# Queries and keys turned and split by the projection, and full-depth score products in the prompt attention

## What the reference computes

```python
def diff_attend(q, k, v, q_pos, k_pos, rel_bias, lam):
    qs = q.reshape(bsz, tq, h, 2, DIFF_DH)          # two maps of 64
    ks = k.reshape(bsz, tk, h, 2, DIFF_DH)
    s = jnp.einsum('bqhmd,bkhmd->bhmqk', qs, ks).astype(F32) * (DIFF_DH ** -0.5)
    rel = q_pos[:, None] - k_pos[None, :]
    bias = jnp.moveaxis(rel_bias.astype(F32)[t5_bucket(rel)], -1, 0)
    s = jnp.where(rel >= 0, s + bias[None, :, None], jnp.finfo(F32).min)
    p = jax.nn.softmax(s, axis=-1)
    a = p[:, :, 0] - lam * p[:, :, 1]
    return jnp.einsum('bhqk,bkhd->bqhd', a, v.astype(F32))
```

## Time and profile before

| what | us |
|---|---|
| median of three runs | 3699.82 (3698.76 to 3701.97) |
| the profiled execution, its own time | 3702.15 |
| span of the profile (first to last instruction) | 3700.1 |
| projection 2, second pass | about 364 |
| prompt attention | about 770 |
| mean granted TensorE clock | 0.967 of full |

### The profile page before, as it was taken

One profiled execution on the slowest core, in us unless ns is written; L12 is line 12 of the kernel. 1 busy time (PEld: TensorE's weight loads), 2 busy tenths in 40 slices (PEclk: granted clock), 3 DMA queues, 4 the chain that ended last, 5 costly groups with the idle time before them and its releaser, 6 DMA issues. The chain is left out here.

```text
span 3700.1 us, 54274 instructions
## 1 busy us (share of the span) xinstructions
PE 3428.9 (93%) x19183; PEld 2764.3 (75%) x19183; DVE 1649.9 (45%) x3504; ACT 1077.4 (29%) x1792; POOL 267.3 (7%) x539
## 2 busy tenths in 40 slices
PE   8999997996899997999999989999999968499999
PEld 6888996774688886888888867777777755278887
DVE  3222201555555553222300028788888733455554
ACT  2111101332211212111200017677777622311111
POOL 0000001110000000000000002112122100000000
PEclk9999998998899999999999989999999978799999
DMA  5433443335322214433422341111111099522221
GB/s 211 150 121 116 142 137 115 119 108 180 135 79 87 78 61 175 153 129 124 149 95 93 104 117 41 45 39 49 48 48 31 14 358 348 199 73 83 80 78 49
DMA packets 218236, 421.99 MB, mean 114 GB/s; under 512 B 20685, under 2 KB 111606, under 8 KB 218054
## 3 DMA queue, kind: packets, MB, share of 16 engines
q1 hardware_dynamic: 218070, 419.89, 32.7%
HBM read 281.51 MB, written 140.14 MB: 114 GB/s over the span
## 5 line engine op out<-in xcount | busy, mean ns | idle before, releaser
L320 PE MATMUL in_ps_y<-in_w_hi,in_x_hi 128*128 128x512 f32 (+2 forms) x2040 | 770.9, 378 | 10.9 <-DVE in_w_lo L423 5.5
L322 PE MATMUL in_ps_y<-in_w_lo,in_x_hi 128*128 128x512 f32 (+2 forms) x2040 | 768.0, 376 | 0.0
L324 PE MATMUL in_ps_y<-in_w_hi,in_x_lo 128*128 128x512 f32 (+2 forms) x2040 | 767.8, 376 | 0.0
L320 PEld LDWEIGHTS in_ps_y<-in_w_hi,in_x_hi 128*128 128x128 f32 x2040 | 384.7, 189 | 75.1 <-issue 11.7
L324 PEld LDWEIGHTS in_ps_y<-in_w_hi,in_x_lo 128*128 128x128 f32 x2040 | 384.4, 188 | 64.1
L322 PEld LDWEIGHTS in_ps_y<-in_w_lo,in_x_hi 128*128 128x128 f32 x2040 | 384.5, 188 | 62.6
L1821 DVE TENSOR_SCALAR_CACHE_REDUCE att_s<-att_ps_s,att_far 128x256 f32<-128x256 f32 (+3 forms) x608 | 331.9, 582 | 34.4 <-PE att_ps_s L1626 30.9
L441 DVE COPY in_out<-in_ps_y 128x512 f32<-128x512 f32 (+1 forms) x85 | 55.8, 657 | 604.9 <-PE in_ps_y L324 604.9
L1664 PEld LDWEIGHTS att_ps_o<-att_v,att_a_t 128*128 128x128 f32 x2176 | 264.2, 191 | 61.8 <-issue 52.0
L1664 PE MATMUL att_ps_o<-att_v,att_a_t 128*128 128x128 f32 x2176 | 308.3, 285 | 0.5 <-ACT att_o L1730 0.5
L1709 ACT ACTIVATE att_s<-att_s,att_shift 128x128 f32<-128x128 f32 (+15 forms) x256 | 306.4, 1199 | 3.4 <-DVE att_shift L1841 3.4
(11 more groups left out here) (246 smaller groups left out, 4731.8 us busy)
## 6 DMA issues: line engine op xcount, KB each, us to landing
smp_k_pg<-in_cache_k SPq DMA_DIRECT2D x64, 512.0 KB, 7.1
smp_v_pg<-in_cache_v SPq DMA_DIRECT2D x64, 512.0 KB, 6.8
x_turned<-in_x_hi SPq DMA_DIRECT2D x34, 512.0 KB, 5.1
x_turned<-in_x_lo SPq DMA_DIRECT2D x34, 512.0 KB, 5.8
factors<-in_out SPq DMA_DIRECT2D x68, 256.0 KB, 2.0
in_x_hi<-x_turned SPq DMA_DIRECT2D x34, 512.0 KB, 4.3
in_x_lo<-x_turned SPq DMA_DIRECT2D x34, 512.0 KB, 5.1
res_factors<-factors SPq DMA_DIRECT2D x34, 512.0 KB
```

The lines of the kernel that those rows point to most:

```text
L320: nc.tensor.matmul(ps_y[g][:, cols], x_hi[u][:, k, :], w_hi[g][:, k, cols], start=(k == 0), stop=False)
L322: nc.tensor.matmul(ps_y[g][:, cols], x_hi[u][:, k, :], w_lo[g][:, k, cols], start=False, stop=False)
L324: mm = nc.tensor.matmul(ps_y[g][:, cols], x_lo[u][:, k, :], w_hi[g][:, k, cols], start=False, stop=(k == KD - 1))
```

## The change

The second pass of projection 2 turns and splits q and k itself. After a group is copied to `out`, PE turns it in four 128x128 transposes into `ps_t` (`turn_again`, placed between two groups of products), ACT writes the high part (scaled for q), DVE the low part, both into halves of the buffers `xt`, which the second pass doesn't use, and SyncE stores both parts turned to four new scratch tensors (1024 x 2048 each; `store_turned`). The stores of q as it is go, but for the samples' tile. In the attention, `prep`, `high`, `low` and `load_nat` go; a head is loaded by twelve DMAs (`load_parts`) into stacked tiles: for each map, `q_hl` holds the high part of q in partitions 0 to 63 and the low part in 64 to 127, `k_hh` the high part of k twice, `k_ll` the low part twice. Scores of a piece are two products of full depth for each map. The handover of scores is by map instead of by pair, and `TURN_RING` becomes 4.

```diff
@@ project
+    def turn_waits(n, t, g):
+        if n == 1 and g in turn:
+            if not (isinstance(t, int) and t == 0):
+                return TURNS * t + g + 1 - TURNS
+        return None
...
+        def re_part(part, n):
+            return xt[part][:, n % 2 * BANK:(n % 2 + 1) * BANK]
...
+                def store_turned(t, g):
+                    sp.wait_ge(re_lo_done, after(TURNS * t + g + 1))
+                    stand_alone(sp, core)
+                    head = turn[g][3]
+                    for part in range(2):
+                        dst = turn[g][part].rearrange("(h p) n -> p h n", p=P)[:, head:head + BANK // P, bass.ds(t * P, P)]
+                        sp.dma_start(dst, re_part(part, g).rearrange("p (h n) -> p h n", n=P)).then_inc(re_kept[g % 2], 16)
+                def stores(n, t):
+                    if n and turn and not (isinstance(t, int) and t == 0):
+                        store_turned(t - 1, G[n] - 1)
+                    for g in range(G[n]):
+                        if not (n and g in turn and not turn[g][4]) or isinstance(t, int) and t == LAST:
+                            store(n, t, g)
+                        if n and turn and g >= 1 and not (isinstance(t, int) and t == LAST):
+                            store_turned(t, g - 1)
...
+                def turn_again(t, g):
+                    n = TURNS * t + g
+                    pe.wait_ge(out_done[g], after(so_far(1, g) + t + 1))
+                    pe.wait_ge(re_lo_done, after(n - 1 if not (isinstance(t, int) and n < 2) else 0))
+                    for b in range(BANK // P):
+                        mm = nc.tensor.transpose(ps_t[g % 2][:, b * P:(b + 1) * P], out[g][:, b * P:(b + 1) * P],
+                                                 core.ident[:, :])
+                    mm.then_inc(re_turned, 1)
...
+                        if n and turn:
+                            if g == 1 and not (isinstance(t, int) and t == 0):
+                                turn_again(t - 1, G[n] - 1)
+                            if g >= 2 and not (isinstance(t, int) and t == LAST):
+                                turn_again(t, g - 2)
...
+                    if n and turn and not (isinstance(t, int) and t == LAST):
+                        turn_again(t, G[n] - 2)
...
+                def high_again(t, g):
+                    act.wait_ge(re_turned, after(n + 1))
...
+                    nc.scalar.activation(re_part(0, g).bitcast(F32R), ps_t[g % 2][:, :], ACT.Copy,
+                                         scale=turn[g][2]).then_inc(re_hi_done, 1)
...
+                def low_again(t, g):
+                    dve.wait_ge(re_hi_done, after(n + 1))
+                    nc.vector.scalar_tensor_tensor(re_part(1, g).bitcast(F32R), ps_t[g % 2][:, :], turn[g][2],
+                                                   re_part(0, g), ALU.mult, ALU.subtract).then_inc(re_lo_done, 1)
@@ attention
-    SLOTS, ROW_RING, TURN_RING = 5, 4, 8
+    SLOTS, ROW_RING, TURN_RING = 5, 4, 4
...
-        k_hi = [sb(f"k_hi{u}", [P, SEQ], F32R) for u in range(2)]
-        k_lo = [sb(f"k_lo{u}", [P, SEQ], F32R) for u in range(2)]
-        q_hi = [sb(f"q_hi{u}", [P, SEQ], F32R) for u in range(2)]
-        q_lo = [sb(f"q_lo{u}", [P, SEQ], F32R) for u in range(2)]
+        k_hh = [[sb(f"k_hh{u}{m}", [P, SEQ], F32R) for m in range(2)] for u in range(2)]
+        k_ll = [[sb(f"k_ll{u}{m}", [P, SEQ], F32R) for m in range(2)] for u in range(2)]
+        q_hl = [[sb(f"q_hl{u}{m}", [P, SEQ], F32R) for m in range(2)] for u in range(2)]
...
+                def load_parts(h, u):
+                    for m in range(2):
+                        for dst, (top, low) in ((q_hl, q_parts), (k_hh, (k_parts[0], k_parts[0])),
+                                                (k_ll, (k_parts[1], k_parts[1]))):
+                            for half, src in enumerate((top, low)):
+                                sp.dma_start(dst[u][m][half * D_DH:(half + 1) * D_DH, :].bitcast(F32),
+                                             src[bass.ds(h * D_VD + m * D_DH, D_DH), :]).then_inc(parts_in[u], 16)
...
-                for g in range(4):
-                    load_nat(0, g)
+                load_parts(0, 0)
                 load_head(0, 0)
-                for g in range(4):
-                    sp.wait_ge(s["turned"], after(2 * g + 2))
-                    load_nat(1, g)
...
                         sp.wait_ge(s["piece_free"], after(PIECES * H + SLOTS))
                         stand_alone(sp, core)
+                        load_parts(H + 1, 1 - u)
                         load_head(H + 1, 1 - u)
                     for i in range(T):
...
-                        if i % 4 == 3 and not (isinstance(H, int) and H + 2 >= D_HEADS):
-                            sp.wait_ge(s["turned"], after(PREPS * (H + 1) + i // 2 + 1))
-                            stand_alone(sp, core)
-                            load_nat(H + 2, i // 4)
...
-                    if c == 0:
-                        pe.wait_ge(s["lo_done"], after(PREPS * H + 2 * (i // 4 + 1)))
-                    pe.wait_ge(s["piece_free"], after(PIECES * H + 2 * at + 2))
-                    for q_part, k_part in ((q_hi, k_hi), (q_hi, k_lo), (q_lo, k_hi)):
-                        for m in range(2):
-                            rows = slice(m * D_DH, (m + 1) * D_DH)
+                    if at == 0:
+                        pe.wait_ge(parts_in[u], after(need_parts(H, u)))
+                    for m in range(2):
+                        pe.wait_ge(s["piece_free"], after(PIECES * H + 2 * at + m + 1))
+                        for k_part in (k_hh, k_ll):
                             mm = nc.tensor.matmul(ps_s[(2 * at + m) % SLOTS][:, 0:hi_ - lo_],
-                                                  q_part[u][rows, i * P:(i + 1) * P], k_part[u][rows, lo_:hi_],
-                                                  start=(q_part is q_hi and k_part is k_hi), stop=(q_part is q_lo))
-                    mm.then_inc(s["piece_ready"], 1)
+                                                  q_hl[u][m][:, i * P:(i + 1) * P], k_part[u][m][:, lo_:hi_],
+                                                  start=(k_part is k_hh), stop=(k_part is k_ll))
+                        mm.then_inc(s["piece_ready"], 1)
```

More of the change, by code:

```diff
@@ L50 @@
 REV = 384
+HEAD_SCALE = -(D_DH ** -0.5)
 class Core:
@@ L122, in so_far, with kept_tiles @@
         return TILES * sum(g < G[a] for a in range(n))
+    turn = turn or {}
+    TURNS = len(turn)
+    def kept_tiles(g):
+        return 1 if g in turn and not turn[g][4] else TILES
+    def turn_waits(n, t, g):
[3 more added lines that the diff above has]
+        return None
     with ExitStack() as mem:
@@ L224, in later_pass @@
                     load_again(t + 1, u)
-                    for g in range(G[n]):
-                        store(n, t, g)
+                    stores(n, t)
                 load_x(0, 0)
@@ L269, in _ @@
                 load_again(1, 0)
-                for g in range(G[1]):
-                    store(1, 0, g)
+                stores(1, 0)
                 with sp.Fori(0, TILES // 2 - 1) as j:
@@ L275, in _ @@
                 later_pass(1, TILES - 2, 1)
-                for g in range(G[1]):
-                    store(1, LAST, g)
+                stores(1, LAST)
                 if beside:
@@ L280, in _ @@
                 for g in range(SLOTS):
-                    sp.wait_ge(stored[g], after(16 * so_far(NP, g)))
+                    sp.wait_ge(stored[g], after(16 * (so_far(1, g) + (kept_tiles(g) if g < G[1] else 0))))
+                for i in range(2 if turn else 0):
+                    sp.wait_ge(re_kept[i], after(32 * LAST * TURNS // 2))
             @block.gpsimd
@@ L398, in _, with again_tile @@
                         weights_high(first_piece[1] + 2 * g + 1)
-                with act.Fori(0, TILES) as t:
+                def high_again(t, g):
+                    n = TURNS * t + g
+                    act.wait_ge(re_turned, after(n + 1))
+                    first = isinstance(t, int) and t == 0
+                    act.wait_ge(re_kept[g % 2], after(0 if first and g < 2 else 32 * (TURNS // 2 * t + g // 2)))
+                    nc.scalar.activation(re_part(0, g).bitcast(F32R), ps_t[g % 2][:, :], ACT.Copy,
+                                         scale=turn[g][2]).then_inc(re_hi_done, 1)
+                def again_tile(t):
                     for g in range(G[1]):
                         evict(1, t, g)
+                        if turn and g == 0 and not (isinstance(t, int) and t == 0):
+                            high_again(t - 1, G[1] - 1)
+                        if turn and g >= 1 and not (isinstance(t, int) and t == LAST):
+                            high_again(t, g - 1)
+                again_tile(0)
+                with act.Fori(1, LAST) as t:
+                    again_tile(t)
+                again_tile(LAST)
             @block.vector
@@ L1486, in bank_uses @@
                 break
```

(23 more changed lines are left out.)

87 lines of the change are left out of this document (41 added, 46 removed).

## The result

The changed kernel takes 3916.47 us (median of four runs, 3911.01 to 3922.61) against 3699.29 beside it: ratio 1.0585, interval 1.0573 to 1.0598, slower by 217 us. 3877 was forecast, +177.5; the time lies outside the forecast's own stretch (3845 to 3905), inside the range (3735 to 3945), and nearest to the rival *half the ports* (3933). The profiled execution took 3922.61 us, its span is 3920.9.

A forecast was written before the change was run, and what follows sets the result against it. It took the projection's second pass as bound by PE alone and prompt attention as mixed, PE or DVE by rows. 28.5 - 40 + 48 + 109 + 22 + 10 = +177.5 us gave 3877; range 3735 to 3945.

The forecast's parts named there:

- half the ports: Rival, chance 0.20: the attention's loads of 64 partitions move only 210 GB/s; total +233 us, time 3933.
- part 1: Second pass of the second projection: 256 transposes added to PE, paid uncovered; +28.5 us.
- first load of the attention: First head's start: loading parts, v and bias at 273 GB/s delays the attention; +13.8 us.
- parts 2 and 3: Attention: four full-depth score products replace six, and turning inside it goes; -5 us a head, -40 in all.
- part 4: Rows 12 to 15 of each head: PE waits for ACT's copies in the smaller ring; +6 us a head, +48.
- part 5: Attention: row 2's output waits for row 0's store behind the loads; 18.1 us a head, +109 in six heads.
- clock after the stalls: Attention: PE restarts at half clock after each stall, an estimated 1.5 us each; +10 us.
- Stores pass the loads: Rival, chance 0.09: stores in the attention aren't held behind loads, so no stall; +50 us, time 3750.
- full rate: Rival, chance 0.14: the attention's loads move 418 GB/s, stalls are shorter; total +116 us, time 3816.
- doesn't do what it says: Rival without its own chance: full-depth score products run no faster, losing 3 us a head; +20 on any case.
- Faster: Rival, chance 0.09: attention rows win back PE and DVE time with the ring's wait hidden; -42 us, time 3658.
- The sign for being wrong: Attention: output waits under 5 us a head, or rows without a stall shorten by over 6 us a head.

The follow-up runs named there:

- e9: Only the projection's turning, splitting and storing of q and k, with the attention of the kernel before: 3731.65 us, ratio 1.0076 to the kernel before.
- e1: Changed kernel with the next head's twelve half loads spread behind the stores of rows 0 to 9: 3731.88 us, ratio 1.0088 to the kernel before.
- e6: Changed kernel with both the loads spread over the rows and five tiles in the ring: 3670.39 us, ratio 0.9918 to the kernel before.
- e8: e6 with the score products of the kernel before (six of 64 rows) and their four loads: 3677.21 us, ratio 0.9938 to the kernel before.
- e3: Changed kernel with five tiles of turned probabilities in the ring instead of four: 3846.10 us, ratio 1.0395 to the kernel before.
- e10: Changed kernel with v, bias and far of heads 1 to 7 issued ahead of the twelve half loads instead of behind them: 3918.18 us.

## Why the prediction was right, and where it was not

The direction and the chain of causes were right: the stall, its place and its releaser, the ring's bubbles and the uncovered turns. The sizes were not, and the time fell outside the forecast's own 3845 to 3905. By steps:

| step | forecast, us | measured, us |
|---|---|---|
| part 1, turns in the projection | +28.5 | +30.6 (trace), +29.7 (e9) |
| first load of the attention | +13.8 | +19.6 |
| parts 2 and 3, over all heads | -40 | about -82 |
| part 4, ring of 4 | +48 | +61.5 (e1 to e6) |
| part 5, held stores | +117 | +184.6 (changed to e1) |
| clock after the stalls | +10 | not seen behind the stalls |
| sum | +177.5 | +217 in the runs; these rows give 213 |

The -82 is made from heads of before and e6: 9.6 in the first (row 0 to row 15), six times 11.8, 2.2 in the last. The +19.6 is from the first load to the first output, 44.9 against 25.3; most of what it has over the forecast is the rate, below. Beside the runs that are set against each other the kernel before took 3697.8 to 3702.8, so these rows are good to a few us.

**The rate** is the step of part 5 that failed. I took 273 GB/s as the mean of three half-microseconds, and they were peaks; the longer stretch, 210 over 2.5 us, was the right row and stood as a rival with 0.20. At 221, v and the parts take 33.8 us, the store lands 36.6 after the first load, and a head pays 118.82 - 90.86 = 28.0 where I had 18.1. About 7 us of the 10 are the rate; row 2 was also due 2.3 us sooner after that load (6.1 instead of 8.4), in part because prep is gone, and the slack behind the stall (a mean wait of 29.3 in heads 1 to 6) is 29.3 - 28.0 = 1.3 instead of 2.6. The sentence of the Trainium skill (SBUF — State Buffer, "Door 1: The DMA port swizzle" and "Can I just issue two DMAs to hit both halves?") that I weighed beside a rival, on half of the ports and on two loads to the two halves, is borne out: the halves alternate between the two sides of the partitions here and still move 221 GB/s, somewhat above its 196 at 1 MB, and 415 to 428 come only with loads over all 128.

**Parts 2 and 3** were mis-sized the other way. Part 2 is right, 3.6 us a head against 3. Part 3's own share, the other 2 of the 5 us a head, is the step that failed: prep was not a sum of PE's and DVE's shares: from before to e8, which keeps the half-depth products, a head falls by 8.2. The rows tell why: rows 8, 10 and 13 come 9.02, 10.03 and 6.25 us after the row before them in the old kernel and 7.17, 8.17 and 4.75 in e8, while rows 9 and 11 don't move. There a chain across three engines (turn, high part, low part, bank free) stood in the row's way. e8's ring is 5 instead of 8, its loads are others and its scores are handed over by map, so this is an argument from rows, not an isolated test.

**Part 4** held in mechanism (e3) and was 8.1 us a head instead of 6; PE's waits for the copies are 6.0 of that (47.9 in eight heads). **The clock** does stand at 1.2 GHz until about 2415.2, four microseconds behind PE's first product, but row 3's output comes 3.12 us behind row 2's, as in e1's same head without a stall, and rows 3 to 15 together take 81.0 us against 82.0 (means of heads 1 to 6). So nothing of it shows there, unless it is in the 1.3 us by which the slack fell short; the 3.7 us in the last head were not in the forecast.

**The rivals.** "Stores pass the loads" is excluded by e10, "full rate" by the windows, "doesn't do what it says" by e8. "Half the ports" named the rate. "Faster" is a real part of the picture: with stores free and one tile more in the ring, the attention wins back more than the projection pays (e6). The sign for being wrong, rows without a stall over 6 us a head shorter than before, stayed unmet only because the smaller ring took 8.1 us back: a head without its stall is 3.7 shorter than before (90.9 in e1 against 94.5), and 11.8 in e6, more than the 9.5 of *faster*. Two of the rivals' sums were slightly off: full rate comes to +114 by its own terms, not 116, and 3 us in eight heads are 24, not 20; neither moves the range. What I looked for as long landings of the store showed as a late issue instead (23.5 us in L1662); e10 makes it a long landing, at the same cost. Two errors of opposite sign, 42 us too little gain and 90 too little loss (less the clock's 10), partly cancelled. That is luck: 40 us off in the sum is better than the steps were.

## What to carry to other kernels

A load moved to one place has to be costed with everything that is issued behind it on its queue: ask which buffer's release waits for the first store in line, and spread the loads over the rows if one does. Take a transfer's rate from the longest stretch of the trace that has its shape, not from the fastest. A ring that shrinks to exactly one row's groups turns a loose dependence into a lockstep; one tile of slack took PE's waits from 47.9 to 2.0 us.

## What the hardware showed that I had not expected

- The issue of a DMA can hold its engine: 23.54 us for the bias behind v and twelve halves, 1.34 us behind v alone (e1). An issue's cost depends on what its queue still holds; in e10, with v and the bias ahead of the halves, the bias took 1.23. How much it takes to hold the engine no run here tells.
- A load with an outermost count of 2 ran on two engines: 53 GB/s, against 428 for the same bytes with 64 outermost.
- A small store on another engine's queue passes 7.5 MB of loads in part: 11.1 us of waits in a head instead of 30.5, the longest landing 14.8.
- The DMA share reads 1.0 at 221 GB/s as at 428: a full share doesn't say that the rate is the best to be had.
- The clock of TensorE fell in a stretch in which PE waited half of the time (busy 2.93 of the 6 us before): 1.2 GHz for 10 us in the changed kernel's last head, which took 3.7 us more, where the same waits in e1 left it at 2.4.
